# Attention's small products of three heads put side by side behind one weight half, turned maps all in PSUM bank 7

## What is computed

```python
proj = h @ w_in[l]
(qm, km, vm, om, zm, im, fm, qa, ka, va, za, gm, ga) = jnp.split(proj, split_idx, axis=-1)
...
# diff_attention(q, k, v, lam, rel_bias), per block of 128 queries and per head, causal:
logits = jnp.einsum('bhmqd,bhmkd->bhmqk', qh[:, :, :, q0:end], kh[:, :, :, :end])
p = jax.nn.softmax(logits + bias[None, :, None], axis=-1)
a = p[:, :, 0] - lam * p[:, :, 1]
outs.append(jnp.einsum('bhqk,bhkd->bhqd', a, vh[:, :, :end]))
...
ha = head_rmsnorm(ha.reshape(B, S, A_V_WIDTH), A_HEADS, anorm_g[l]) * (1.0 - lam_init)
```

## Time and profile before

| | |
|---|---|
| time, median of 3 runs | 1560.87 us (1558.64 to 1560.92) |
| span of the profiled execution | 1556.7 us |
| what the runs take beyond that span | 1.9 us (fastest) to 4.2 us (median) |
| PE busy | 1199.0 us, 77% |
| DVE, ACT busy | 614.5 us, 426.0 us |
| granted TensorE clock up to about 700 us | full |
| DMA from about 630 us on | about 430 GB/s |

### The profile page before, as it was taken

One profiled execution on the slowest core, in us unless ns is written; L12 is line 12 of the kernel. 1 busy time (PEld: TensorE's weight loads), 2 busy tenths in 40 slices (PEclk: granted clock), 3 DMA queues, 4 the chain that ended last, 5 costly groups with the idle time before them and its releaser, 6 DMA issues.

```text
span 1556.7 us, 18205 instructions
## 1 busy us (share of the span) xinstructions
PE 1199.0 (77%) x7368; PEld 694.3 (45%) x7368; DVE 614.5 (39%) x1041; ACT 426.0 (27%) x644; POOL 39.0 (3%) x64
## 2 busy tenths in 40 slices
PE   7999999999999999975665665675665666655675
PEld 6888977887887899621211111111111111111122
DVE  3786789889777877511011011011011011010111
ACT  3666357786564664300000000000000000000001
POOL 0100000010001000000000000000000000000000
PEclk9999999999999999988777777878877787788778
DMA  9877877686655666999999999999999999999996
GB/s 359 283 264 229 300 257 245 221 313 221 231 177 197 216 229 263 395 422 430 430 431 431 431 431 432 432 432 431 430 431 431 430 431 432 432 430 431 431 431 276
DMA packets 78195, 550.51 MB, mean 354 GB/s; under 512 B 5032, under 2 KB 5352, under 8 KB 61856
## 3 DMA queue, kind: packets, MB, share of 16 engines
q1 hardware_dynamic: 75024, 541.08, 86.0%
q0 software_dynamic: 2800, 7.97, 1.7%
q10 hardware_dynamic: 288, 0.30, 0.1%
HBM read 548.24 MB, written 1.61 MB: 353 GB/s over the span
## 4 chain that ended last, share of the span: by engine, by line
PE 46%; DMA 35%; DVE 12%; ACT 4%; issue 3%; DVEq 0%; ACTq 0%; POOL 0%; SPq 0%
PE ps L603 43%; DMA b<-in_w_down 34%; DVE b L1528 6%; PE ps L607 3%; ACT b L1164 3%; DVE b L1545 2%; DVE b L2258 1%; ACT b L1166 1%; DVE b L2199 1%; DMA b<-in_w_in 1%; DVE b L2205 1%; DMA b<-in_const 0%; DVE b L1538 0%; DVE b L1559 0%; DVE b L2239 0%
## 5 line engine op out<-in xcount | busy, mean ns | idle before, releaser
L603 PE MATMUL ps<-b,b 128*32 128x512 f32 (+7 forms) x6922 | 1129.9, 541 | 303.2 <-DMA b<-in_w_up 117.3
L603 PEld LDWEIGHTS ps<-b,b 128*32 128x32 f32 (+2 forms) x6922 | 637.6, 159 | 756.7 <-issue 450.1
L1164 ACT ACTIVATE b<-ps 128x512 f32<-128x512 f32 (+3 forms) x165 | 92.3, 559 | 874.9 <-PE ps L603 576.1
L1528 DVE TENSOR_TENSOR b<-b,b 128x1024 fp32r<-128x1024 f32 (+5 forms) x254 | 277.1, 1091 | 94.9 <-ACT b L1164 75.7
L1164 ACT ACTIVATE b<-b 128x1024 fp32r<-128x1024 f32 (+6 forms) x219 | 219.1, 1001 | 211.2 <-PE ps L603 164.5
L2248 DVE TENSOR_TENSOR b<-b,ps 128x512 f32<-128x512 f32 x16 | 11.0, 688 | 393.2 <-issue 379.9
L2258 DVE TENSOR_TENSOR b<-b,ps 128x1024 f32<-128x1024 f32 x28 | 34.2, 1222 | 311.2 <-PE ps L603 311.2
L607 PE MATMUL ps<-b,b 128*128 128x128 f32 (+1 forms) x360 | 70.0, 323 | 38.7 <-DVE b L1559 23.5
L607 PEld LDWEIGHTS ps<-b,b 128*128 128x128 f32 (+1 forms) x360 | 46.1, 169 | 89.1 <-DVE b L1559 36.4
L1545 DVE SCALAR_TENSOR_TENSOR b<-b,b,b 128x512 f32<-128x512 f32 (+3 forms) x50 | 63.2, 1263 | 4.3 <-ACT b L1164 0.5
L1528 DVE TENSOR_TENSOR b<-ps,b 128x512 f32<-128x512 f32 (+8 forms) x69 | 37.6, 545 | 27.4 <-PE ps L603 15.9
(11 more groups left out here) (60 smaller groups left out, 203.7 us busy)
## 6 DMA issues: line engine op xcount, KB each, us to landing
b<-in_w_gate SPq DMA_DIRECT2D x30, 4096.0 KB, 42.7
b<-in_w_up SPq DMA_DIRECT2D x30, 4096.0 KB, 43.2
b<-in_w_down SPq DMA_DIRECT2D x29, 4096.0 KB, 38.2
b<-in_w_in SPq DMA_DIRECT2D x73, 1024.0 KB, 5.4
b<-in_w_ada SPq DMA_DIRECT2D x28, 1024.0 KB, 5.3
b<-in_w_down SPq DMA_DIRECT2D x5, 2048.0 KB, 13.9
b<-in_w_ada SPq DMA_DIRECT2D x16, 512.0 KB, 11.4
b<-in_w_proj_m SPq DMA_DIRECT2D x8, 1024.0 KB, 5.3
```

What stands on the lines that cost most here:

```text
L603: return e.matmul(o, lhsT, rhs, start=start, stop=stop, skip_group_check=True)
L1164: e.activation(o, i, f, bias=bias, scale=scale).then_inc(mark[0], 1)
L1528: e.tensor_tensor(o, a, b, op).then_inc(mark[0], 1)
```

## The change

On PE, values, scores and turning now stand together behind half (s, 0), in this order, of heads s - 15, s - 12 and s - 14. ACT's copy of the turned map moves with the turning, from (s, 3) with head s - 13 to (s, 2) with head s - 14; its copy and squares of the values stay at (s, 1), one head later. The turned maps of all heads go to bank 7; before, those of heads 0 to 4 shared bank 6 with the values. The sum `R2` in bank 7 moves on by two halves, and so does DVE's read of it. DVE's `mean(assq, ...)` of the attention's squares goes from (22, 0) to (22, 2).

```diff
-ADA_SUM = {(13, 0): "R3", (17, 0): "R2", (26, 0): "R4"}
+ADA_SUM = {(13, 0): "R3", (17, 2): "R2", (26, 0): "R4"}
...
-    misc = {4: [], 5: [], 6: [], 7: ["R00", "R01", "R1", "R3", "R2", "FL5", "FL6", "FL7", "R1F", "R4"]}
+    misc = {4: [], 5: [], 6: [], 7: ["R00", "R01", "R1", "R3", "FL0", "FL1", "FL2", "FL3", "R2", "FL4", "FL5", "FL6", "FL7", "R1F", "R4"]}
...
-        misc[6] += [f"FL{h}"] * (h < 5) + [f"AV{h}"]
+        misc[6].append(f"AV{h}")
...
# tensor engine
-                if 14 <= s < 22 and c == 0:
-                    attn_values(s - 14)
-                if 13 <= s < 21 and c == 2:
-                    attn_flips(s - 13)
-                if 12 <= s < 20 and c == 1:
-                    attn_scores(s - 12)
+                if 15 <= s < 23 and c == 0:
+                    attn_values(s - 15)
+                if 12 <= s < 20 and c == 0:
+                    attn_scores(s - 12)
+                if 14 <= s < 22 and c == 0:
+                    attn_flips(s - 14)
                 if (s, c) == (21, 2):
                     bank = begin("R1F")
...
# scalar engine
-                if 14 <= s < 22 and c == 1:
-                    h = s - 14
+                if 15 <= s < 23 and c == 1:
+                    h = s - 15
                     e.wait_ge(*full(f"AV{h}"))
...
-                if 13 <= s < 21 and c == 3:
-                    h = s - 13
+                if 14 <= s < 22 and c == 2:
+                    h = s - 14
                     e.wait_ge(*full(f"FL{h}"))
                     copy(AT[h % 2], ps[:, USE[f"FL{h}"][0], 0:3 * P], to=free(f"FL{h}"))
...
# vector engine
-                if (s, c) == (17, 1):
+                if (s, c) == (17, 3):
                     mod_rows(2, "R2", MODT[1])
...
-                if (s, c) == (22, 0):
+                if (s, c) == (22, 2):
                     e.wait_ge(*free(f"AV{AH - 1}"))
                     mean(assq, 2 * ADH)
```

## The result

After the change the kernel takes 1563.11 us (median of 17 runs, 1561.99 to 1565.15), beside 1560.50 us of the kernel before (17 runs on the same chip, 1557.59 to 1562.92). The ratio is 1.0021 with a 95% interval of [1.0013, 1.0028]: slower by 3.3 us, 2.0 to 4.4.

A forecast was written before the change was run, and what follows sets the result against it. PE was taken to set the pace in the first part, shifts there reaching the end in full. R1F 3.7 us later, plus 0.7 for values, less 0.6 absorbed, gave 3.8 on 1560.87: 1564.7 us, range 1560.8 to 1567.0.

The forecast's parts named there:

- the forecast's 3.8 us: Delay in slots 22 to 24: R1F 3.7 later, plus 0.7 for head 7's values, less 0.6 no longer waited.
- The shift passes to the end: A shift in the first part, where PE works without a gap, passes to the end in full.
- PE's gain, 0.7 us: Joining saves 0.10 us in each of five steps (slots 15 to 19), 0.06 in three others; bounds 0 and 3.6.
- The place: R1F in bank 7 behind half (21, 2) decides: it waits until ACT has copied out head 7's turned map.
- The chain to load 44, -0.54 us: ACT's chain from head 6's exponentials to load 44 runs 0.54 us earlier, since a map copy moves away.
- The context tokens, +0.3 us: POOL's 1 MB load meets the end of load 44 and delays it by 0.3 us (0 to 2.4).
- `R1F` 3.7 us later, a wait of 4.5 us: R1F starts near 328.2 instead of 324.51 us; PE, there near 323.7, waits some 4.5 us for ACT's copy.
- The 0.6 us before the second turning of `HM` absorbed: PE comes at 363.0 us, after the gatings near 360.7, so today's 0.6 us wait there goes.
- The clock: Rival: 2.1 us of short matmuls lower the clock to 1.2 GHz for the half behind; +13.6, 1578 us; chance 0.02.
- What a wait is worth: At R1F the 3.7 us delay counts in full towards the end, less 0.6 us before HM's second turning.
- The rival without a wait, 1560.2 us: No wait at R1F if the copy is done by 323.7 us, so PE's 0.7 us gain counts; chance 0.14.

The follow-up runs named there:

- bank 4: The changed kernel with R1F put in bank 4, behind the scores of head 7, instead of bank 7; 1560.78 us, ratio 1.0002 [0.9993, 1.0011].

## Why the prediction was right, and where it was not

Sign and size came out (forecast 1564.7, measured 1563.1, and 1560.87 x 1.0021 = 1564.1 by the ratio). The mechanism is half right, and the runs show which half. That the size fits is in good part luck: the forecast's 3.8 us were all waiting, with nothing for the clock; the runs give the wait about 0.5 us and the clock some 2 us. One term too high and one left out nearly cancelled.

- **The shift passes to the end:** right. From the 1000th matmul on the change needs 1131.1 us, before 1130.0.
- **PE's gain, 0.7 us:** mis-sized a little. A step with three pieces saves 13.07 - 12.91 = 0.16 us, not 0.10. That it is lost in a wait was right. Why most of the passage between the pieces stays, which the forecast puts down to the rows of the array that the scores use, no run shows.
- **The place:** right. `R1F` waits for ACT's copy, behind two high parts and load 44, and bank 7 alone makes the wait, as bank 4 showed.
- **The chain to load 44, -0.54 us:** too small. ACT's high part came at 321.01 instead of 322.62, 1.6 us earlier. 0.8 of it is a shift of the whole trace from ahead of the change (the 250th matmul at 206.60 instead of 207.36); the other 0.8 is the chain. The exponentials of head 6 moved by 1.0 us on the same count. 0.54 of it is the copy that left; for the rest, the maxima that they wait for come some 0.4 us earlier (ACT now idles 1.23 us for them), which fits PE's gain but was not tested apart.
- **The context tokens, +0.3 us:** nothing. They were issued at 317.67, 1.65 us behind load 44, which landed in 5.0 us.
- **`R1F` 3.7 us later, a wait of 4.5 us:** measured 2.3 (3.0 without the shift) and 3.92 us. The two terms above make most of the difference.
- **The 0.6 us before the second turning of `HM` absorbed:** right, it is gone, and PE came there at 362.94, forecast 363.0.
- **The clock:** the step that failed. The rival asked whether short matmuls let it fall, and gave it 0.02. The idle time itself let it fall (granted 0.70 and 0.50 behind it in the two traces of the change, 1.00 with the wait filled), and no term stood for that. It cost 1.0 us in one trace and 2.5 in the other.
- **What a wait is worth:** failed too. I counted the 3.7 us in full, less 0.6. But take it away, and PE waits 3.0 us for `HM`, since ACT, POOL and DVE are late in any case. The wait costs 0.3 to 0.5 us of the stretch (198.98 with the clock kept against 198.66 and 198.46) and the fallen clock 1.4 to 2.8 us.
- **The rival without a wait, 1560.2 us:** its kernels measured 1.0001 and 1.0002 times before. No change can be told, and a gain of 0.7 us would lie within these intervals. The traces speak against it: DVE's second gating comes later than before, and PE waits for it.

The nine kernels without the long wait, or with it filled, lie between 0.9999 and 1.0011, and all but that with `R1F` later have 1 in their intervals. None can be told to be faster than the kernel before. Joining's gain of some 0.8 us is smaller than the 1.4 us to which a ratio is known, so the times neither show it nor exclude it.

**Open:** the trace of before has only 0.53 us of waits before `HM`, and a stretch of 196.1 us, while kernels whose times cannot be told from it have 1.4 to 3.0 us of waits and stretches of 196.7 to 198.7. Its own time lies under its median, but there is no second trace of it, so whether it usually waits more is not known. What decides whether the clock falls at the 1.95 us wait, and whether it costs 1.0 or 2.5 us behind the 3.9 us one, was not controlled.

## What to carry to other kernels

Before a wait is priced, ask what PE would wait for without it: if the next consumer is set by other engines, the wait moves and costs next to nothing, and so does a saving in front of it. Then ask whether the waits, one by one, are long enough to lower the clock, since two shorter ones of 3 us together (1.88 and 1.09) left the clock up here, where one of 3.9 us did not, nor did one of 2.38 or of 2.28 us. When pieces of work are gathered at one place, follow the last one of the series to its neighbours: what it now shares a bank with, and on which side of a load's landing its work on the other engines falls.

## What the hardware showed that I had not expected

- The clock fell to its lower level in one idle stretch of 3.0 to 5.9 us between long runs of matmuls, in all four traces that have one. It fell behind the one wait of 2.38 us and the one of 2.28 us, and not behind two of 1.88 and 1.89 us. After 1.95 us it fell in five of fourteen, in kernels that are alike there: 1.6 us by chance, from one execution to the next. And in two of fourteen it fell near 126 us with PE busy throughout. The Trainium skill, TensorE: Matmul & The Clock Gate, section "Loop structure matters more than you think", warns that a long wait for a DMA between matmuls lowers the clock; these traces agree, though here ACT waits for the DMA and PE only stands behind ACT.
- 16 small matmuls of no use in the wait (3.73 us of PE's time) kept the clock and won back most of the loss: 1.0004 against 1.0021 and 1.0016.
- One load of 1 MB in the same kernel, issued at the same point of the program, landed in 4.9 us in one execution and in over 7.5 in another (316.99 to 324.8), and PE's wait behind it was 3.0 or 5.9 us.
